# A transformer layer with routed experts: remainders of the weights formed two units ahead, raw ring of two buffers, last expert step by itself

## What is computed

```
logits = t @ w_router + b_router               # t: 1024 tokens x 1024
top_val, top_idx = top_k(logits, 4)            # of 32 experts
top_w = softmax(top_val)
for each expert e, for its tokens:
    hu  = t @ w1[e] + b1[e]                    # 1024 -> 2048
    glu = min(hu[:, 0::2], 7); lin = clip(hu[:, 1::2], -7, 7)
    act = glu * sigmoid(1.702 * glu) * (lin + 1)
    y  += top_w * (act @ w2[e] + b2[e])        # 1024 -> 1024
x = x + ga2 * rmsnorm(y, g_post_ffn)
```

## Time and profile before

| | |
|---|---|
| median of 3 runs | 2715.78 us (2714.61 to 2716.11) |
| the profiled execution, its own time | 2711.47 us |
| its span | 2709.4 us |
| TensorE matmul busy | 2511.5 us, 93% |
| TensorE weight load busy | 1966.8 us, 73% |
| VectorE busy | 1914.2 us, 71% |
| ScalarE busy | 1506.5 us, 56% |
| GpSimd busy | 403.8 us, 15% |
| weight loads of the experts | 448 of 1024 KB, 6.4 us to landing (median) |

### The profile page before, as it was taken

One profiled execution on the slowest core, in us unless ns is written; L12 is line 12 of the kernel. 1 busy time (PEld: TensorE's weight loads), 2 busy tenths in 40 slices (PEclk: granted clock), 3 DMA queues, 4 the chain that ended last, 5 costly groups with the idle time before them and its releaser, 6 DMA issues. The chain is left out here.

```text
span 2709.4 us, 38802 instructions
## 1 busy us (share of the span) xinstructions
PE 2511.5 (93%) x12226; PEld 1966.8 (73%) x12227; DVE 1914.2 (71%) x2595; ACT 1506.5 (56%) x1841; POOL 403.8 (15%) x302
## 2 busy tenths in 40 slices
PE   7999969999979749999999999999999999999967
PEld 2466549999967637777777777777888888888852
DVE  2541337777766468888888888877768777777866
ACT  3210126666654146767777776666656666666752
POOL 1000011312212111112020211102102210210220
PEclk8999979999989769999999999999999999999988
DMA  9641032424233168999898989888778878877978
GB/s 345 149 140 63 1 111 72 97 61 104 65 120 130 70 235 316 329 322 344 302 361 300 356 301 349 310 291 321 269 277 315 296 254 303 321 259 274 363 287 320
DMA packets 298373, 643.79 MB, mean 238 GB/s; under 512 B 12322, under 2 KB 13570, under 8 KB 298162
## 3 DMA queue, kind: packets, MB, share of 16 engines
q1 hardware_dynamic: 279890, 574.44, 61.7%
q0 software_dynamic: 18432, 68.70, 7.2%
HBM read 604.40 MB, written 44.65 MB: 240 GB/s over the span
## 5 line engine op out<-in xcount | busy, mean ns | idle before, releaser
L1724 DVE TENSOR_TENSOR w_lo_x<-wring_x,w_hi_x 128x2048 fp32r<-128x2048 f32 x446 | 1010.2, 2284 | 44.3 <-issue 13.7
L1579 ACT ACTIVATE w_hi_x<-wring_x 128x2048 fp32r<-128x2048 f32 x448 | 850.9, 1911 | 73.6 <-DMA wring_x<-in_w_mlp 72.3
L1930 PE MATMUL psum<-w_hi_x,x_hi_x 128*128 128x512 f32 x992 | 415.3, 419 | 12.4 <-DVE w_lo_x L1724 12.4
L1932 PE MATMUL psum<-w_hi_x,x_lo_x 128*128 128x512 f32 x992 | 388.7, 392 | 0.0
L1931 PE MATMUL psum<-w_lo_x,x_hi_x 128*128 128x512 f32 x992 | 388.4, 392 | 0.0
L1927 PE MATMUL psum<-w_hi_x,x_both_x 128*128 128x512 f32 x640 | 270.8, 423 | 0.0
L1544 POOL TENSOR_TENSOR poolgate_x<-poolgate_x 128x1 f32<-128x1 f32 x62 | 62.7, 1012 | 1277.2 <-DVE y_x L1769 842.8
L1928 PE MATMUL psum<-w_lo_x,x_both_x 128*128 128x512 f32 x640 | 250.6, 392 | 0.0
L1930 PEld LDWEIGHTS psum<-w_hi_x,x_hi_x 128*128 128x128 f32 x992 | 188.5, 190 | 54.4 <-DVE w_lo_x L1724 20.8
L1932 PEld LDWEIGHTS psum<-w_hi_x,x_lo_x 128*128 128x128 f32 x992 | 186.9, 188 | 41.7
L1931 PEld LDWEIGHTS psum<-w_lo_x,x_hi_x 128*128 128x128 f32 x992 | 187.8, 189 | 35.9
(11 more groups left out here) (329 smaller groups left out, 3971.5 us busy)
## 6 DMA issues: line engine op xcount, KB each, us to landing
wring_x<-in_w_mlp SPq DMA_DIRECT2D x448, 1024.0 KB, 6.4
bias<-bias_d SPq DMA_DIRECT2D x32, 640.0 KB, 7.8
late<-in_w_ada SPq DMA_DIRECT2D x32, 512.0 KB, 3.8
yg<-y_d SPq DMA_DIRECT2D x32, 512.0 KB, 9.8
ring<-in_w_ada SPq DMA_DIRECT2D x4, 2048.0 KB, 8.4
ring<-in_w_in SPq DMA_DIRECT2D x4, 2048.0 KB, 9.8
ring<-in_w_out SPq DMA_DIRECT2D x2, 2048.0 KB
mix_d<-o SPq DMA_DIRECT2D x16, 256.0 KB, 2.0
```

Of the source, the lines that this page charges most:

```text
L1579: act.activation(w_hi[:, u % HI, k, :], ring[:, u % RING, k, :], ACT.Copy).then_inc(hi_done, 1)
L1724: dve.tensor_tensor(w_lo[:, u % LO, k, :], ring[:, u % RING, k, :], w_hi[:, u % HI, k, :].bitcast(F32), ALU.subtract).then_inc(lo_done, 1)
L1930: pe.matmul(bank, hi[:, k, :], w_hi[:, u % HI, k, :], start=(not biased and k == 0), stop=False)
L1932: last = pe.matmul(bank, lo[:, k, :], w_hi[:, u % HI, k, :], start=False, stop=(k == KD - 1))
```

## The change

- The raw ring has two buffers instead of three, w_lo three instead of two. VectorE forms remainders of unit n+2 while the products of unit n run, so in the same period in which ScalarE rounds that unit; at the start it forms those of both first units.
- In VectorE's triple the first remainder piece of the tile's second unit is put ahead of add_up or add_output of r=1, the second piece behind it. ScalarE's order stays.
- The last single step is taken out of the loop and runs as a body without a next step: no loads, gather, transposes, rounding or remainders for one. The constants of the routing (thirds, single count, bound of the triples) are moved by one to fit.
- The softmax weights and by_expert are computed at the start of experts, and b_mlp2 is loaded there behind btab; VectorE waits for it together with the bias table. combine loses these parts, and TensorE's wait for the rows with them.

```diff
-    table[:, THIRDS:THIRDS + E] = 3 * np.arange(E) + 5
+    table[:, THIRDS:THIRDS + E] = 3 * np.arange(E) + 6
@@ middle, vector
-            link(dve.scalar_tensor_tensor(rest[:, 1:2], rest[:, 0:1], -1.0, pairs[:, 1:2], ALU.add, ALU.min))
+            link(dve.scalar_tensor_tensor(rest[:, 1:2], rest[:, 0:1], -2.0, pairs[:, 1:2], ALU.add, ALU.min))
...
-            dve.tensor_tensor(K.table[:, SINGLE_COUNT:SINGLE_COUNT + 1], at[0:1, 2, E - 1:E], triples[:, 1:2], ALU.subtract)
+            dve.scalar_tensor_tensor(K.table[:, SINGLE_COUNT:SINGLE_COUNT + 1], at[0:1, 2, E - 1:E], -1.0, triples[:, 1:2], ALU.add, ALU.subtract)
@@ experts
-    RING, CH = 3, 2
-    HI, LO = 3, 2
+    RING, CH = 2, 2
+    HI, LO = 3, 3
@@ program
-            return Step(SINGLE, single, both, triple)
+            last = Step(SINGLE, single, both, triple)
+            body(last, None)
+            return last
@@ gpsimd
             pool.dma_start(btab[:, :], K.btab_d).then_inc(bias_loaded, 16)
+            pool.dma_start(K.bias2[:, :], io["b_mlp2"][0]).then_inc(bias_loaded, 16)
@@ scalar
+            act.wait_ge(weighed, 1)
+            act.activation(exps[:, :, :], expd[:, :, :], ACT.Exp).then_inc(weighed, 1)
             first = Step(SINGLE, 0, 0, 0)
@@ vector
+            dve.tensor_tensor(expd[:, :, :], K.top[:, :, 0:TOPK], K.top[:, :, 0:1].to_broadcast([P, T, TOPK]), ALU.subtract).then_inc(weighed, 1)
+            dve.wait_ge(weighed, EXPS)
+            link(dve.tensor_reduce(norm[:, :, 0:1], exps[:, :, :], AX.X, ALU.add))
+            link(dve.reciprocal(norm[:, :, 1:2], norm[:, :, 0:1]))
+            link(dve.tensor_tensor(K.weights[:, :, :], exps[:, :, :], norm[:, :, 1:2].to_broadcast([P, T, TOPK]), ALU.mult))
...
-            dve.wait_ge(bias_loaded, 32)
+            dve.wait_ge(bias_loaded, 48)
...
-            for c in range(CH):
-                piece(first, 0, c)
+            for u in range(2):
+                for c in range(CH):
+                    piece(first, u, c)
@@ vector, single and pair (both pieces)
-                    ahead(st, nxt, n + 1, 0)
+                    ahead(st, nxt, n + 2, 0)
@@ vector, triple
-                    ahead(st, nxt, 2 * n + 1, 0)
+                    ahead(st, nxt, 2 * n + 2, 0)
...
-                    ahead(st, nxt, 2 * n + 1, 1)
+                    ahead(st, nxt, 2 * n + 2, 1)
                     if n < UP:
                         columns(st, 2 * n)
+                    wait_products_before(dve, st, n, 2)
+                    ahead(st, nxt, 2 * n + 3, 0)
+                    if n < UP:
                         add_up(st, n, 1)
                     else:
                         add_output(st, n, 1)
-                    wait_products_before(dve, st, n, 2)
-                    ahead(st, nxt, 2 * n + 2, 0)
-                    ahead(st, nxt, 2 * n + 2, 1)
+                    ahead(st, nxt, 2 * n + 3, 1)
@@ combine, gpsimd
-            pool.dma_start(bias[:, :], io["b_mlp2"][0]).then_inc(rows_loaded, 16)
@@ combine, tensor
-            pe.wait_ge(routed, BY_MADE)
...
-            pe.wait_ge(spread_out, BY_COPIED)
-            pe.wait_ge(rows_loaded, 48)
+            pe.wait_ge(by_copied, 1)
@@ combine, scalar
-            act.wait_ge(routed, EXPD)
-            act.activation(exps[:, :, :], expd[:, :, :], ACT.Exp).then_inc(spread_out, 1)
-            act.wait_ge(routed, WEIGHTS)
@@ combine, vector: the softmax and by_expert go
-            dve.wait_ge(rows_loaded, 48)
+            dve.wait_ge(rows_loaded, 32)
```

More of the change, by code:

```diff
@@ L1509, in body @@
             def body(st, kind):
-                nxt = st.then(kind)
-                chosen, chosen_next = experts_of(sp, st, counts[0]), experts_of(sp, nxt, counts[0])
+                chosen = experts_of(sp, st, counts[0])
                 for u in range(2, st.units):
                     load(st, u, chosen)
-                load(nxt, 0, chosen_next)
-                load(nxt, 1, chosen_next)
+                if kind:
+                    nxt = st.then(kind)
+                    chosen_next = experts_of(sp, nxt, counts[0])
+                    load(nxt, 0, chosen_next)
+                    load(nxt, 1, chosen_next)
             program(counts, sp, body)
@@ L1546, in body @@
             def body(st, kind):
-                nxt = st.then(kind)
+                ahead = 2 if kind else 0
                 pool.wait_ge(gate_open, 4 * st.steps + 2)
                 pool.wait_ge(gathered, 16 * (st.blocks + st.R))
[L1550 to L1556, removed]
+                if kind:
+                    nxt = st.then(kind)
+                    pool.tensor_copy(token[:, 0:nxt.R], slots(K.token_of, nxt)).then_inc(gate_open, 1)
+                    pool.wait_ge(gate_open, 4 * st.steps + 3)
+                    pool.wait_ge(xt_done, st.blocks + st.R)
+                    gate()
+                    gather(nxt)
+                    pool.wait_ge(gate_open, 4 * st.steps + 4)
                 pool.wait_ge(y_stored, 16 * st.blocks + 16)
@@ L1559, in body @@
                 pool.tensor_copy(y_row[:, 0:st.R], slots(K.row_of, st)).then_inc(gate_open, 1)
-                pool.wait_ge(gate_open, 4 * st.steps + 5)
+                pool.wait_ge(gate_open, 4 * st.steps + 3 + ahead)
                 pool.wait_ge(y_copied, DOWN * st.steps + DOWN)
@@ L1654, in single @@
                         columns(st, n - 1)
-                    if n - UP in range(nxt.R):
+                    if nxt and n - UP in range(nxt.R):
                         rows(nxt, n - UP)
@@ L1706, in body @@
             def body(st, kind):
-                (single, pair, triple)[st.kind - 1](st, st.then(kind))
+                (single, pair, triple)[st.kind - 1](st, st.then(kind) if kind else None)
             program(counts, act, body)
@@ L1942, in body @@
             def body(st, kind):
-                nxt = st.then(kind)
+                nxt = st.then(kind) if kind else None
                 pe.wait_ge(sel_up_ready, st.steps + 1)
@@ L1987, in combine @@
         stat = sb("stat5", [P, T, 3])
[L1988 to L1989 removed]
+        weights, by_expert, bias = K.weights, K.by_expert, K.bias2
         diag = sb("diag5", [P, 2, TOPK - ON_PE, P])
[L1991 to L1994, removed]
+        by_copied = sem("by_copied")
         byT = sb("by_expert_T", [E, T, P])
```

72 lines of the change are left out of this document (38 added, 34 removed).

## The result

| | before | after |
|---|---|---|
| median | 2715.2 us (4 runs) | 2837.7 us (4 runs, 2834.9 to 2842.0) |
| ratio | | 1.0456, 95% interval 1.0440 to 1.0473 |
| span of the profiled execution | 2709.4 us | 2837.8 us |
| mean granted clock of TensorE | 0.962 | 0.951 |

A forecast was written before the change was run, and what follows sets the result against it. The prediction took the expert stage as TensorE's, with ScalarE, VectorE and DMA just behind. Its terms, 58 + 25 + 18 + 4.5 - 4 - 1 = +100.5, on 2715.8 gave 2816 us, range 2762 to 2860.

The forecast's parts named there:

- The triple's order: Triple steps: a remainder ahead of the add of product r=1 delays bank and gate, 9.7 us per step, 58 us.
- the walk: Timed chain through one triple tile: TensorE waits 1.9 us for the bank and 1.1 for the gate, period about 17.0.
- Single behind a triple: Single steps after triples: late y add, two remainders before the first gate and a late load, 4.1 x 6 = 25 us.
- Single behind a pair: Single steps after pairs: remainder after a late rounding delays the gate, 2.3 us each, times 8: 18 us.
- the same with milder loads: Single steps after pairs: the reasoning for singles after triples, with ScalarE waiting 1.31 us for a load; 18 us.
- My bound for all single steps: All 17 single steps together: from 0, if late loads are rare, to 88 us; 47 taken.
- The clock: Rival, chance 0.12: stalls in the 6 singles after triples also lower TensorE's clock, 24 us more, 2840.
- Double buffering: Single steps: two raw buffers are enough, so their term is 0; leads to the 2769 us rival, chance 0.13.
- Pair steps, counts, head (0): Pair steps hide the remainder in idle time, loop counts balance, routing work moved to the expert stage's head costs 0 to 1.
- Combine and last step: At the end: combine without routing work and gain row wait, -4; last single step without preparing another, -1.
- Only the bank wait: Rival, chance 0.13: single steps stay as they are and the triple's 58 us remains, 2769 us.
- Faster: Rival, chance 0.09: in triples the bank is free within 3.9 us, no tile stalls, w_lo waits go; 2683 us.

The follow-up runs named there:

- The half loads: The changed kernel with every weight load behind the first two units moving only the first half of its rows: 2783.6 us.
- the full ring: The kernel before with only routing weights, b_mlp2 and last step changed; three raw buffers, one unit ahead, old order: 2706.7 us, ratio 0.9975.

## Why the prediction was right, and where its sum was off

- *The triple's order (58, measured 57.6).* Both links of the walk are in the trace: 2.0 us at the bank (forecast 1.9) and 1.3 at the gate (forecast 1.1), period 16.8 (forecast 17.0). The stall before the second down tile (forecast 1.9) is there too. Putting the add first removed the one, putting the gate first most of the other.
- *Single behind a triple (25, measured 22.9).* Size right, in part by luck. I gave 1.5 us to the order at the border, 1.9 to a load of 10.6 us and nothing to the clock, and saw two stalls. The trace has one, of 4.8 us. The half loads give back only 1.5 of the 3.8 us, and the stall stays. Behind it TensorE works for about 3.2 us at 0.50, which by my estimate (half of that time) is 1.6 of the 3.8.
- *Single behind a pair (18, measured 47.5).* This is the term that failed. The step "the same with milder loads" took the landings of the kernel before as given. With two raw buffers a load starts when the rounding and the remainder of the same period are done; a late one makes the next late, and landings of 8.3 to 11.3 us in a row end in a stall of 4.0 us. The half loads show the cause (40.5 us), the two raw buffers in the old kernel show it again without the new order (48.9). My bound for all single steps, 0 to 88, held it (72); the value taken, 47, was too near the row of the triple part. I had also priced the ring at its first late load, with nothing for the second.
- *The clock.* I held the falling clock for a rival at 0.12, put it behind the triples and left it out of the sum. It fell in 16 stretches between 1000 and 2700 us, against one in the kernel before: behind the stalls of all six singles behind a triple and of seven of the eight behind a pair, in the first single, and in two triples. TensorE is busy for 63 us in these stretches. Half of that, some 30 us, is my estimate of the loss; about 17 of it lie in the 47.5 of the singles behind a pair. So the rival's condition came true, in part at other places, and its 2840 is nearer to the measured 2838 than my 2816. By the same estimate the waits alone cost some 13 us behind the triples, where I had 25, and some 31 behind the pairs, where I had 18: these two errors nearly cancelled, and that is luck.
- *Double buffering.* The Trainium skill (Trainium Kernel Development and Optimization, Best Practices) asks for double buffering so that transfers overlap compute. Read as a rule that two raw buffers are enough, it would have left the single steps as they were. The measurement decides against that reading here (2895.2 us with two raw buffers and nothing else): a turn of the ring takes a load, its rounding and its remainder, and with two buffers these have to end within two product periods.
- *Pair steps, counts, head (0):* +0.9, the same mix, and 21.6 us from routing to x_lo in both. *Combine and last step (-5):* -4.9 in the changed kernel, where the last single has its own losses, and -7.3 with the full ring.
- *Rivals.* "Only the bank wait" would be 2769, and both other links are in the trace. "Faster" fell at the point that it named: the bank was free 2.0 us too late. What I didn't see is that this part of the change, with the old buffers, is a gain of 13 us: I had costed order and buffers only together.

## What to carry to other kernels

An order of work is good or bad only with the state of its inputs: the same remainder ahead of the same add gains where the piece lies ready and stalls the next engine where it has to be made first. When a buffer is taken out of a ring, count what must happen in one turn of it (issue, landing, conversion, release) against the periods that the turn now spans, with the late landings and not the median one, and ask what the second late load does. A change of several parts deserves its parts one by one: here two of three were gains (-22 us together) inside a change that cost 122.

## What I had not expected of the hardware

Stalls of 1.3 and 2.0 us, three of each in every triple, left TensorE's clock alone. Windows of two tiles of the changed kernel:

```profile
1188.00:1205.00 17.00, 14.49 (x65) 11.23 (x65) 12.68 (x13) 10.09 (x11) 0.00 (x0) 1.00 0.71 250
1205.00:1222.00 17.00, 14.53 (x65) 11.26 (x65) 12.82 (x13) 10.09 (x11) 0.00 (x0) 1.00 0.69 247
```

The one of 4.0 us shown above was followed by 0.50, the 1.2 GHz level. But the length of a single stall doesn't decide it. Two more windows of the same kernel, each right behind a stall of the weight loads: of 2.28 us until 1253.29 (second down tile of a triple), and of 3.58 us until 2047.77 (single behind a pair):

```profile
1254.00:1258.00 4.00, 4.00 (x13) 3.13 (x12) 3.60 (x3) 1.77 (x1) 0.00 (x0) 0.57 0.98 367
2048.00:2052.00 4.00, 4.00 (x20) 3.29 (x19) 3.78 (x3) 3.17 (x4) 0.00 (x0) 1.00 1.04 358
```

The shorter one was followed by the half level (13 matmuls in 4 us instead of 20), the longer one was not. Of the six stalls of 2.3 us at that place in the triples two were followed by it, four were not. So gaps of the same sum can cost differently: most short ones here cost their own length, most of the long ones another 2 us or so, and which of them do so can't be told from the length alone.
